# Two fused transformer blocks on one core: linears dealt out over the steps of two attentions, and two orders in layer norm

## Chip, core and metric

One core of a Trainium2 chip runs the whole program. The metric is the device time of one execution in microseconds. Matmuls run on TensorE (PE; its weight loads are PEld), the other engines are VectorE (DVE), ScalarE (ACT), GpSimd (POOL) and SyncE (SP), which issues the DMAs.

## What is computed

Two blocks run one after the other on x of 512 tokens by 1024 channels, all in float32. The change lies in the second block, which has two layers (l = 0, 1). What matters of each, cut from the reference:

```python
proj = x @ w_in
da_q, da_k, da_v, hg_q, hg_ff, hg_fb, hg_i, hg_g, mx_q = jnp.split(proj, split_idx, axis=-1)
...
p = jax.nn.softmax(s, axis=-1)               # differential attention, 4 heads, 512 keys
a = p[:, :, 0] - lam * p[:, :, 1]
return jnp.einsum('bhqk,bkhv->bqhv', a.astype(v.dtype), v)
...
mkv = (mem @ w_mem_kv).reshape(B, M, 2, MX_HEADS, MX_HEAD_DIM)
mx_o = memory_attention(mx_q.reshape(B, S, MX_HEADS, MX_HEAD_DIM), mkv[:, :, 0], mkv[:, :, 1])
...
mix = jnp.concatenate([da_o, hg_o, mx_o], axis=-1) @ w_out
x = layer_norm(DEEPNORM_ALPHA * x + mix, ln1_g, ln1_b)
...
return layer_norm(DEEPNORM_ALPHA * x + ffn, ln2_g, ln2_b)
```

`hg_o` comes from a gated linear recurrence over the tokens, whose inputs are the hg parts of the projection. The memory has 256 rows.

## The kernel before

**Linears.** A float32 product is made of three faster matmuls. A weight block of 128x1024 lands in a ring of nine slots, ACT casts it to its high part WH (`cast_to`, L431), POOL subtracts to get the low part WL (`rest_to`, L442), and PE multiplies WH by the high and low parts of the input and WL by the high part (L490, L491, L493 in `unit_pe`; L468 to L470 where two groups run side by side in `pair_pe`). WH and WL have three places each (`SPLITS`), so the cast of block p waits until PE has used block p - 3. A group of a feature linear is one block: eight values of k, three matmuls of 512 columns each, into one PSUM bank, 24 matmuls in all.

**Order.** Each engine's program is written out by hand in `tensor`, `vector`, `scalar`, `gpsimd` and `sync`, and an engine takes its instructions in that order. Semaphores tie them together. PSUM has eight banks. `bank.take` gives out the one that was taken longest ago, and `bank.claim` sets some aside for a pool of their own, from which `take_in` takes.

**A layer.** `tok_pe` makes q, k and v and turns q and k (L2413), and ACT (L2426) and DVE (L2443) copy the turned tiles. Then comes the differential attention, `diff`: 16 tiles (head by 128 queries) in a pipeline of 20 steps. In step t PE does the values of tile t - 4 (L2485), the turn of tile t - 3 (L2478) and the scores of tile t (L2471). DVE takes the maxima (L2494, L2496) and mixes the two softmaxes (L2499 to L2505), ACT does the two exponentials (L2517), the copy of the turned tile (L2524) and of the values (L2529). Beside it, in every fourth step (`t % 4 == 0`), one whole item of `mem_pe` is put in: for l = 0 first the values of the memory (`mem_values_pe`, L2558), then the four groups of the memory queries (`L_mq`), whose PSUM ACT copies at L2587.

Then `memory`, the attention to the memory: 16 tiles, 19 steps, three short PE stages each: values (L2349), turn (L2322), scores (L2288). DVE takes the maximum (L2294, L2301) and scales the output (L2359, L2362), ACT does the exponential (L2311) and the copy of the turned tile (L2331). Beside it DVE also normalises the differential attention's output (`da_norm_v`, L2629 to L2640, one piece a step for ten steps). PE has nothing beside it. All its scores wait until the last group of queries has been copied (`A.ready`).

Then `recur_in_pe`: twelve groups (`L_hg`) for the recurrence, back to back, whose results ACT puts through silu (L2756) and sigmoid (L2758) and DVE through `gates_v` (L2716 to L2727). The recurrence, the output linear (`mix`), a layer norm, the feed forward part and a second layer norm follow.

**Layer norm.** There are five: `ln_in`, and two a layer. In `spread_v` DVE forms the variance (L881, L884), ACT takes the root (L725) and copies the mean (L896), DVE takes the reciprocal (L887), PE spreads it to all partitions (`whole_pe`, L714), and DVE scales X (L781). The mean is first taken off X: DVE does that for tiles 0 and 1 (`off_v`, L874), POOL for tiles 2 to 7 (L901). `kept_a` (L804) adds the bias to the kept copy of X on ACT, after the high parts (L798). For three of the five, PE has the memory's keys (L2544) or values to compute around L714. For the first norm of layer 1 and the last norm it has nothing.

## Time and profile before

| | before |
|---|---|
| median of 3 runs | 3335.7 us (3334.98 to 3341.27) |
| profiled execution, its own time | 3338.81 us |
| its span, first to last instruction | 3337.0 us |
| TensorE busy | 3234.9 us (97%) |
| weight load / VectorE / ScalarE / GpSimd busy | 77% / 42% / 39% / 40% |
| mean granted TensorE clock | 0.988 |
| DMA | 286.10 MB, mean 86 GB/s |

Busy PE time counts a matmul from its start to a modelled end, and the ends overlap the next start, so the pitch from start to start says more than the duration of one. A bracket at the end of a timeline row is the idle time before it and what ended it.

### The profile page before, as it was taken

How to read it: one execution, taken by the hardware profiler on the slowest of the kernel's cores; microseconds unless marked ns; L12 is line 12 of the kernel's file. 1: busy time of each engine (PE TensorE's matmuls, PEld its weight loads, DVE VectorE, ACT ScalarE, POOL GpSimd, SP SyncE). 2: the span in 40 equal slices, each digit the busy share in tenths (PEclk: the TensorE clock that was granted, in tenths of full speed). 3: DMA queues.
4: the chain of work that ended last, by engine and by line, in shares of the span. 5: the costliest groups of instructions: out<-in, count | busy, mean ns of one | idle time of the engine just before them, and what ended most of it. 6: DMA issues, size and time to landing. Idle time of an engine off the chain costs nothing.

```text
span 3337.0 us, 40463 instructions
## 1 busy us (share of the span) xinstructions
PE 3234.9 (97%) x16396; PEld 2575.0 (77%) x16396; DVE 1409.0 (42%) x2583; ACT 1306.1 (39%) x2312; POOL 1328.1 (40%) x754
## 2 busy tenths in 40 slices
PE   7999999999998999999999899999999999999998
PEld 4866888888874556888886688888887678878886
DVE  5657332222238773321224676242322658344132
ACT  4222332322245664433333535343333543444243
POOL 2221432222243445444552134644455123554446
PEclk9999999999999999999999999999999999999999
DMA  6144222122132001323232020423333111122321
GB/s 253 53 170 183 101 79 74 51 67 70 47 124 87 13 13 53 137 85 111 77 125 71 32 72 9 153 89 100 96 92 111 50 51 52 54 88 81 112 84 56
DMA packets 85639, 286.10 MB, mean 86 GB/s; under 512 B 9771, under 2 KB 10347, under 8 KB 84940
## 3 DMA queue, kind: packets, MB, share of 16 engines
q1 hardware_dynamic: 85452, 283.50, 25.9%
q8 instruction: 130, 2.13, 0.3%
q14 instruction: 57, 0.47, 0.0%
HBM read 281.37 MB, written 2.10 MB: 85 GB/s over the span
## 4 chain that ended last, share of the span: by engine, by line
PE 89%; DVE 6%; ACT 2%; DMA 1%; issue 1%; POOL 0%; SPq 0%; DVEq 0%; ACTq 0%
PE ps L490 21%; PE ps L493 21%; PE ps L491 21%; PE ps L530 2%; PE ps L532 2%; PE ps L531 2%; PE ps L2037 2%; PE ps L2849 1%; PE ps L2107 1%; PE ps L1270 1%; PE ps L2471 1%; PE ps L2485 1%; PE ps L559 1%; PE ps L468 1%; PE ps L469 1%
## 5 line engine op out<-in xcount | busy, mean ns | idle before, releaser
L442 POOL TENSOR_TENSOR WL<-ring,WH 128x1024 fp32r<-128x1024 f32 (+2 forms) x427 | 922.2, 2164 | 1458.0 <-ACT WH L431 1457.7
L490 PE MATMUL ps<-HX,WH 128*128 128x512 f32 x1768 | 694.9, 393 | 3.5 <-POOL WL L442 3.5
L493 PE MATMUL ps<-HX,WL 128*128 128x512 f32 x1768 | 691.7, 391 | 0.0
L491 PE MATMUL ps<-HX,WH 128*128 128x512 f32 x1768 | 690.2, 390 | 0.0
L431 ACT CAST WH<-ring 128x1024 fp32r<-128x1024 f32 (+2 forms) x443 | 420.2, 950 | 374.9 <-PE ps L493 316.8
L490 PE MATMUL ps<-FR,WH 128*128 128x512 f32 x1120 | 418.7, 374 | 0.3
L491 PE MATMUL ps<-FR,WH 128*128 128x512 f32 x1120 | 409.5, 373 | 0.0
L490 PEld LDWEIGHTS ps<-HX,WH 128*128 128x128 f32 x1768 | 332.4, 188 | 82.2 <-issue 6.5
L493 PE MATMUL ps<-FR,WL 128*128 128x512 f32 x1120 | 389.2, 373 | 0.0
L493 PEld LDWEIGHTS ps<-HX,WL 128*128 128x128 f32 x1768 | 333.7, 189 | 49.5
L491 PEld LDWEIGHTS ps<-HX,WH 128*128 128x128 f32 x1768 | 332.7, 188 | 49.3
L954 DVE SCALAR_TENSOR_TENSOR T<-ps,pv,T 128x511 f32<-128x511 f32 (+1 forms) x154 | 109.4, 710 | 499.4 <-ACT T L950 499.3
L490 PEld LDWEIGHTS ps<-FR,WH 128*128 128x128 f32 x1120 | 210.3, 188 | 46.8 <-DVE FR L3062 1.1
L491 PEld LDWEIGHTS ps<-FR,WH 128*128 128x128 f32 x1120 | 210.3, 188 | 37.5
L950 ACT ACTIVATE T<-ps,pv 128x512 f32<-128x512 f32 (+1 forms) x154 | 113.1, 749 | 303.5 <-PE ps L493 290.8
L493 PEld LDWEIGHTS ps<-FR,WL 128*128 128x128 f32 x1120 | 198.6, 188 | 29.8
L909 DVE SCALAR_TENSOR_TENSOR X<-ps,mod,X 128x512 f32<-128x512 f32 x64 | 48.0, 751 | 337.6 <-PE ps L493 320.7
L1593 ACT CAST FR<-T 128x512 fp32r<-128x512 f32 x110 | 61.3, 577 | 248.3 <-DVE T L1621 145.7
L491 PE MATMUL ps<-HC,WH 128*128 128x256 f32 x504 | 141.6, 281 | 0.0
L493 PE MATMUL ps<-HC,WL 128*128 128x256 f32 x504 | 141.4, 281 | 0.0
L490 PE MATMUL ps<-HC,WH 128*128 128x256 f32 x504 | 141.4, 280 | 0.0
L530 PE MATMUL ps<-WH,HX 128*128 128x512 f32 x320 | 126.8, 396 | 0.8 <-ACT AR L2565 0.8
(386 smaller groups left out, 5038.9 us busy)
## 6 DMA issues: line engine op xcount, KB each, us to landing
ring<-in_w_mod SPq DMA_DIRECT2D x96, 512.0 KB, 6.2
ring<-in_ffn_w_up SPq DMA_DIRECT2D x88, 512.0 KB, 3.4
ring<-in_w_up SPq DMA_DIRECT2D x88, 512.0 KB, 3.5
ring<-in_w_in_tok SPq DMA_DIRECT2D x40, 512.0 KB, 3.6
ring<-in_w_in_feat SPq DMA_DIRECT2D x32, 512.0 KB, 3.4
ring<-in_ffn_w_down SPq DMA_DIRECT2D x32, 384.0 KB, 3.1
ring<-in_w_out SPq DMA_DIRECT2D x32, 384.0 KB, 3.1
ring<-in_w_down SPq DMA_DIRECT2D x32, 384.0 KB, 3.2
```

The costliest lines, as they stand in the source:

```text
L431: act.copy(WH[:, p % SPLITS, 0:n], ring.ap(r)).then_inc(*split.a.up("high", p))
L442: pool.tensor_tensor(WL[:, p % SPLITS, 0:n], ring.ap(r), WH[:, p % SPLITS, 0:n], ALU.subtract).then_inc(*ring.frees(r, split.g, "low", p))
L490: pe.matmul(o, high, xh, first, False)
L491: pe.matmul(o, high, xl, False, False)
L493: m = pe.matmul(PS[bs[i]][:, 0:N], low, get(k)[0], False, last)
L530: pe.matmul(PS[bs[t]][:, :], xh[:, tt], high, k == 0, False)
L531: pe.matmul(PS[bs[t]][:, :], xh[:, tt], low, False, False)
L532: m = pe.matmul(PS[bs[t]][:, :], xl[:, tt], high, False, k == 7)
L950: act.activation(dst, src, ACT.Identity, scale=w1, bias=b).then_inc(*steps.up("conv", *name))
L954: dve.scalar_tensor_tensor(dst[:, 1:N], src[:, 0:N - 1], w0, dst[:, 1:N], ALU.mult, ALU.add).then_inc(*steps.up())
L1593: act.copy(hidden(L, n, s)[0], d).then_inc(*fw.a.up("high", L.name, n, s))
L2037: pe.matmul(PS[b][:, 0:c1 - c0], QT[n % 2][0:96, h, t * 128:t * 128 + 128], KT[n % 2][0:96, h, c0:c1], True, True).then_inc(*att.pe.up("sc ...
```

## The change

Six edits, all in how work is ordered:

1. `diff` takes a table `PIECES[l]` that says how many pieces of the work beside it PE does in each of its 20 steps. A piece is one k of a group (three matmuls, `unit_pieces_pe`) or, for l = 0, one of eight pieces of the memory's values. The table of layer 0 gives 2, 1, 1, 1, 1, 1, 1, 0, 2, 2, 2, 2, then 3 a step, 40 pieces in all; that of layer 1 gives 1 to 3 a step, 32 in all. ACT takes its part of a group one step after PE has finished it (`filled`). The scores have a pool of four banks, the work beside two.
2. `memory` gets the first three of the recurrence's twelve groups beside it (`recur_first_pe`), two pieces a step in steps 0 to 7 and one in steps 8 to 15. Their three banks are set aside until the recurrence's input stage, where `recur_in_pe` does the other nine. ACT casts one more block in each of the steps 5, 12 and 18 (`recur_casts_a`).
3. Scores of the memory attention wait for their own head's queries alone (`A.ready(i)`).
4. In `tok_a` the last cast stands behind the four copies of turned keys, and in `mem_a` the cast stands behind the copy and reaches one block further.
5. In `spread_v` DVE takes the reciprocal ahead of the first `off_v`.
6. For the first norm of layer 1, `kept_a` casts two blocks after its first three tiles (`casts` = 2).

```diff
+        def unit_pieces_pe(pe, L, g, stream, b):
...
+            for k in range(k1):
...
+                pe.matmul(o, WH[:, p % SPLITS, c], xh, k == 0, False)
+                pe.matmul(o, WH[:, p % SPLITS, c], xl, False, False)
+                m = pe.matmul(o, WL[:, p % SPLITS, c], xh, False, k == g.kt - 1)
...
+                yield
...
             for j, (k, s) in enumerate(part_items(sts)):
+                if 3 <= j < 3 + casts:
+                    cast_to(act, ring.cast)
...
-            off_v(dve, q, 0)
             dve.wait_ge(*nm.a.at("root", q.name))
             dve.reciprocal(t, t).then_inc(*nm.v.up("inverse", q.name))
+            off_v(dve, q, 0)
             off_v(dve, q, 1)
...
-                for done in A.ready:
-                    pe.wait_ge(*done)
+                pe.wait_ge(*A.ready(i))
...
-            cast_to(act, g.last + 3)
             for h in range(4):
                 act.wait_ge(*da.pe.at("turn", l, h, 1))
...
+            cast_to(act, g.last + 3)
...
-                    b = bank.take("ds", l, i, d)
+                    b = bank.take_in("ds", "ds", l, i, d)
...
+        PIECES = ((2, 1, 1, 1, 1, 1, 1, 0, 2, 2, 2, 2, 3, 3, 3, 3, 3, 3, 3, 3),
+                  (2, 2, 3, 1, 1, 1, 2, 1, 1, 2, 1, 1, 2, 1, 1, 2, 2, 2, 2, 2))
...
-                if t % 4 == 0:
+                for _ in range(turns[t]):
                     next(beside, None)
...
+        def recur_first_pe(pe, l, ready):
+
+            piece = 0
+            for g in L_hg[l].groups[0:3]:
+                b = bank.take_in("first", L_hg[l].name, g.key, 0)
+                for _ in unit_pieces_pe(pe, L_hg[l], g, (hx, S, ready), b):
+                    piece += 1
+                    if piece > 16 or piece % 2 == 0:
+                        yield
+
+        def recur_casts_a(act, l):
+            for t in range(19):
+                if t in (5, 12, 18):
+                    cast_to(act, L_hg[l].groups[(t - 5) // 6].last + 3)
+                yield
```

On PE in the differential attention of layer 0, the order before has 24 matmuls of a group in one block (the first rows of it, after the scores at L2471):

```order
7002 L2478 MATMUL ps<-ident,AR 128x128 x4
7003 L2471 MATMUL ps<-AR 128x512 x2
7004 L490 MATMUL ps<-HX,WH 128x512
7005 L491 MATMUL ps<-HX,WH 128x512
7006 L493 MATMUL ps<-HX,WL 128x512
7007 L490 MATMUL ps<-HX,WH 128x512
```

In the changed kernel every step has two or three pieces (lines are shifted: L2505, L2498, L2491 are values, turn and scores; L508 to L510 a piece):

```order
7038 L2505 MATMUL ps<-AR 128x128 x4
7039 L2498 MATMUL ps<-ident,AR 128x128 x4
7040 L2491 MATMUL ps<-AR 128x512 x2
7041 L508 MATMUL ps<-HX,WH 128x512
7042 L509 MATMUL ps<-HX,WH 128x512
7043 L510 MATMUL ps<-HX,WL 128x512
7044 L508 MATMUL ps<-HX,WH 128x512
7045 L509 MATMUL ps<-HX,WH 128x512
7046 L510 MATMUL ps<-HX,WL 128x512
7047 L2505 MATMUL ps<-AR 128x128 x4
```

The block of 24 is thus dealt out over several steps. On PE in the memory attention of layer 0, two steps before:

```order
7143 L2349 MATMUL ps<-AR 128x128 x2
7144 L2322 MATMUL ps<-ident,AR 128x128 x2
7145 L2288 MATMUL ps<-AR 128x256
7146 L2349 MATMUL ps<-AR 128x128 x2
7147 L2322 MATMUL ps<-ident,AR 128x128 x2
7148 L2288 MATMUL ps<-AR 128x256
```

and one step of the changed kernel, with the start of the next (L2369, L2342, L2308 are values, turn and scores):

```order
7169 L2369 MATMUL ps<-AR 128x128 x2
7170 L2342 MATMUL ps<-ident,AR 128x128 x2
7171 L2308 MATMUL ps<-AR 128x256
7172 L508 MATMUL ps<-HX,WH 128x512
7173 L509 MATMUL ps<-HX,WH 128x512
7174 L510 MATMUL ps<-HX,WL 128x512
7175 L508 MATMUL ps<-HX,WH 128x512
7176 L509 MATMUL ps<-HX,WH 128x512
7177 L510 MATMUL ps<-HX,WL 128x512
7178 L2369 MATMUL ps<-AR 128x128 x2
```

Six matmuls that stood behind the whole stage now stand in each of its first eight steps, three in each of the next eight. On ACT after the first norm of layer 1 (L817 the high parts, L825 `kept_a`, L971 the first convolution of the feed forward part, L431 a cast), changed kernel:

```order
1548 L817 ACTIVATE HX<-X,pv 128x512 x8
1549 L825 ACTIVATE X<-X,pv 128x512 x3
1550 L431 CAST WH<-ring 128x1024
1551 L825 ACTIVATE X<-X,pv 128x512
1552 L431 CAST WH<-ring 128x1024
1553 L825 ACTIVATE X<-X,pv 128x512 x4
1554 L971 ACTIVATE T<-ps,pv 128x512
```

Before, the eight tiles of `kept_a` stood together and the two casts behind the first silu and the first high part of the feed forward stage. The orders of POOL and SP, their instructions and their number are as they were.

## Rows read from the trace of the kernel before

**Rows 1.** The page: busy time of each engine.

```profile
PE 3234.9 (97%) x16396; PEld 2575.0 (77%) x16396; DVE 1409.0 (42%) x2583; ACT 1306.1 (39%) x2312; POOL 1328.1 (40%) x754
```

**Rows 2.** Stretches, memory attention: window, length, busy of PE, PEld, DVE, ACT, POOL, PEclk.

```profile
1871.00:1903.00 32.00, 24.96 (x131) 17.12 (x130) 26.38 (x100) 15.45 (x50) 0.17 (x1) 0.95 0.00 1
...
2676.00:2708.00 32.00, 25.77 (x130) 18.26 (x130) 26.50 (x100) 15.35 (x50) 0.28 (x1) 0.89 0.01 2
```

**Rows 3.** Timeline of PE, layer 0, differential attention: start, duration, instruction, idle before.

```profile
1788.45 1.13 PE L2471 MATMUL ps<-AR 64*128 64x512 f32 x4 [1.59 <-ACT AR L2426]
1789.51 14.00 PE L2558 MATMUL ps<-ring,CX 128*128 128x512 f32 x32
...
1825.67 1.13 PE L2471 MATMUL ps<-AR 64*128 64x512 f32 x4
...
1828.25 1.13 PE L2471 MATMUL ps<-AR 64*128 64x512 f32 x4
1836.33 1.13 PE L2471 MATMUL ps<-AR 64*128 64x512 f32 x4
...
1870.72 1.03 PE L2288 MATMUL ps<-AR 128*128 128x256 f32 x4
```

**Rows 4.** Timeline of PE, layer 1: start of differential attention, start and end of memory attention.

```profile
2605.78 1.13 PE L2471 MATMUL ps<-AR 64*128 64x512 f32 x4 [1.59 <-ACT AR L2426]
2675.61 1.03 PE L2288 MATMUL ps<-AR 128*128 128x256 f32 x4
...
2707.22 0.48 PE L490 MATMUL ps<-HX,WH 128*128 128x512 f32 x1
...
2709.39 0.39 PE L490 MATMUL ps<-HX,WH 128*128 128x512 f32 x1
...
2710.07 0.39 PE L490 MATMUL ps<-HX,WH 128*128 128x512 f32 x1
```

**Rows 5.** Timeline of PE, layer 0, memory attention: one late step and the end.

```profile
1894.21 0.60 PE L2288 MATMUL ps<-AR 128*128 128x256 f32 x2
1894.84 0.71 PE L2349 MATMUL ps<-AR 128*128 128x128 f32 x4
...
1895.61 0.60 PE L2288 MATMUL ps<-AR 128*128 128x256 f32 x2
...
1902.33 0.48 PE L490 MATMUL ps<-HX,WH 128*128 128x512 f32 x1
```

**Rows 6.** Who PE waited for, 1784 to 1904 us: total, times, longest.

```profile
PE ps L2322 <- ACT AR L2311: 5.6, 7, 2.1
PE ps L2349 <- ACT AR L2331: 1.0, 2, 0.6
```

**Rows 7.** Timeline of ACT, layer 0: cast ahead of key copies; a copy in memory attention.

```profile
1785.31 1.08 ACT L431 CAST WH<-ring 128x1024 fp32r<-128x1024 f32 x1
...
1894.41 0.37 ACT L2331 COPY AR<-ps 128x256 f32<-128x256 f32 x1 [0.55 <-PE ps L2322]
```

**Rows 8.** Timeline of DVE and POOL, layer 0: maxima of two steps, and a low part.

```profile
1828.67 0.17 DVE L2496 TENSOR_SCALAR sm<-sm 128x2 f32<-128x2 f32 x1
...
1831.52 2.24 DVE L2496 TENSOR_SCALAR sm<-sm 128x2 f32<-128x2 f32 x1
...
1831.34 2.40 POOL L442 TENSOR_TENSOR WL<-ring,WH 128x1024 fp32r<-128x1024 f32 x1 [42.52 <-ACT WH L431]
```

**Rows 9.** Timeline of ACT, DVE and PE around the first norm of layer 1.

```profile
2947.93 0.31 ACT L725 ACTIVATE T<-T 128x128 f32<-128x128 f32 x1 [0.62 <-DVE T L884]
...
2949.52 0.94 DVE L887 RECIPROCAL T<-T 128x128 f32<-128x128 f32 x1
...
2975.93 0.80 PE L490 MATMUL ps<-HX,WH 128*128 128x512 f32 x1 [2.67 <-POOL WL L442]
```

**Rows 10.** Timeline of POOL and DVE in the last norm: mean off, and scaling.

```profile
3324.18 7.42 POOL L901 TENSOR_TENSOR X<-X,T 128x512 f32<-128x512 f32 x6 [7.79 <-ACT T L896]
...
3326.93 5.45 DVE L3226 SCALAR_TENSOR_TENSOR X<-X,pv,ps 128x512 f32<-128x512 f32 x8 [0.70 <-PE ps L714]
```

More of the change, by code:

```diff
@@ L494, in unit_pe @@
             m.then_inc(*split.pe.up("used", p))
+        def unit_pieces_pe(pe, L, g, stream, b):
+            (p, k0, k1), = g.units
+            get, N, ready = stream
+            assert ring.next() == p
+            pe.wait_ge(*split.g.at("low", p))
+            pe.wait_ge(*bank.free(L.name, g.key, 0))
+            for k in range(k1):
+                c = slice(k * 128, k * 128 + 128)
+                xh, xl = get(k)
+                for done in ready(k):
+                    pe.wait_ge(*done)
+                o = PS[b][:, 0:N]
+                pe.matmul(o, WH[:, p % SPLITS, c], xh, k == 0, False)
+                pe.matmul(o, WH[:, p % SPLITS, c], xl, False, False)
+                m = pe.matmul(o, WL[:, p % SPLITS, c], xh, False, k == g.kt - 1)
+                if k == g.kt - 1:
+                    m.then_inc(*split.pe.up("used", p))
+                yield
         def linear_pe(pe, L, ins, beside=None, groups=None, front=0):
@@ L2573, in mem_pe @@
             if l == 0:
-                mem_values_pe(pe, l)
-                yield
+                yield from mem_value_pieces_pe(pe, l, [bank.take_in("mq", "mv", l, t) for t in range(2)])
             for g in L_mq[l].groups:
-                linear_pe(pe, L_mq[l], lambda g: [(hx, S, ready)], groups=[g])
-                yield
+                b = bank.take_in("mq", L_mq[l].name, g.key, 0)
+                yield from unit_pieces_pe(pe, L_mq[l], g, (hx, S, ready), b)
         def mem_a(act, l):
@@ L2597, in diff, with filled @@
                         run(stage, t - stage)
-                if t % 4 == 0:
+                for _ in range(turns[t]):
                     next(beside, None)
             last_of(beside)
+        def filled(l):
+            turns, n, ends = [0] * 21, 0, list(range(8, 41, 8))[:5 - l]
+            for t, k in enumerate(PIECES[l]):
+                n += k
+                while ends and n >= ends[0]:
+                    turns[t + 1] += 1
+                    ends.pop(0)
+            return turns
         def mem_attention(l):
@@ L2745, in recur_in_pe @@
         def recur_in_pe(pe, l, ready):
-            linear_pe(pe, L_hg[l], lambda g: [(hx, S, ready)])
+            linear_pe(pe, L_hg[l], lambda g: [(hx, S, ready)], groups=L_hg[l].groups[3:])
         def recur_in_a(act, l):
```

45 lines of the change are left out of this document (27 added, 18 removed).

## Prediction

> **What bounds the kernel now.** I read the page first: PE is busy 97% of the span [rows 1]. A kernel in this state gains only where PE waits, or where its busy time is padded. So I went to the timeline of PE in the stages that the change touches, and read pitch, start to start.
>
> In the differential attention the scores of one step start 2.58 us after those of the step before (1825.67 to 1828.25), and 8.08 us after when a group of 24 matmuls lies between (1828.25 to 1836.33) [rows 3]. So a group costs 5.50. A group by itself takes eight k of 0.68 (2709.39 to 2710.07 [rows 4]), that is 5.44, so going in and out of one costs 0.06. DVE needs 2.85 a step (1828.67 to 1831.52) [rows 8], more than PE's 2.58: without a filler DVE falls behind, and in every fourth step a block of 5.5 us lets it catch up again. The stage starts with a wait of 1.59 for the last copy of turned keys [rows 3, 4].
>
> The memory attention is worst. It takes 31.61 us in either layer (1870.72 to 1902.33, 2675.61 to 2707.22) [rows 3 to 5], and its late steps, the best, take 1.40 (1894.21 to 1895.61) [rows 5]. Even those are bound by a chain: the copy of the turned tile ends at 1894.78 [rows 7] and the values start at 1894.84 [rows 5], 0.63 after the scores, although the scores of two tiles in a row are 1.03 long with their modelled end (the first memory row [rows 3]), so that one tile streams for about 0.43. So PE's own work in a step is about 1.40 - 0.20 = 1.20. The early steps wait longer, 5.6 us in seven waits in layer 0 [rows 6], and the granted clock falls to 0.95 and 0.89 in this stage [rows 2], so parts of it run at 1.2 instead of 2.4 GHz. The recurrence's groups behind it run without a gap. They are ready work next to idle time.
>
> **The change part by part.** No arithmetic goes away. Against the profiled execution (3338.8 us, its span 3337.0 and 1.8 around it), with the median of the runs 3.1 below:
>
> *Start of the differential attention.* The cast moved behind the key copies takes 1.08, of which its successor sees some 0.9 [rows 7]. In each layer the wait of 1.59 shrinks by that: 2 x 0.9 = **1.8**. Bounds 0 and 2 x 1.59 = 3.2. I take 0.9, since the last turned tile then becomes the limit. The moved cast is not needed for two more groups; the queued exponential behind it starts later, but the first exponential also waits for DVE's maximum.
>
> *Differential attention.* Layer 0: from 1788.45 to 1870.72 are 82.3 us [rows 3]. PE's own work is 16 x 2.58 = 41.3, the memory's values 13.9 (the 14.0 row less its overlap), four groups of 5.44 = 21.8, in all 77.0: 5.3 of idle and slow time. Layer 1: from 2605.78 to 2675.61 are 69.8 [rows 4], less 41.3 and 21.8: 6.8. In the changed order every step but one has at least one piece, 0.68 (or 1.75 for a piece of the values), so a step lasts 3.26 or more and DVE's 2.85 fits under it, and the last four steps, which have no scores, have two or three pieces. Gain **12.1**. The pool of two banks left for turn and values adds no wait: each reuses a bank whose copy ACT did a step before, and PE needs that copy anyway.
>
> *Memory attention.* 31.6 less 16 steps of 1.20 = 19.2, less 1.0 for the waits of the last three steps, which have no piece (the two waits for L2331 [rows 6]), gives 11.4 a layer, **22.8**. If 1.40 is PE's own pace, it is 16.4. I take 1.20, for the copy that ends just ahead of the values. The three groups' 16.4 us only change place. With two pieces a step lasts 2.56, with one 1.88, and the chain maximum, exponential, turn, copy has that time beside it. The softer wait for the queries matters little, but lets the first scores go while the last queries are copied.
>
> *Going in and out.* PE now visits the filler 19 + 20 + 32 = 71 times instead of 9. 62 x 0.06 = **-3.7** [rows 3]. Bounds 0, and 0.16 a visit (9.9), from the first matmul behind the scores, whose row of 0.48 stands against 0.39 of its followers [rows 4, 5], with 0.06 on top.
>
> *POOL against DVE.* One DVE instruction of 0.17 takes 2.24 in the step in which POOL forms a low part for 2.40 [rows 8]. So each low part can cost DVE 2.1. The Trainium skill ("SBUF — State Buffer", on the port pair that VectorE and GpSimd share) says that the pair is an exclusive lock held for the whole instruction, and the row agrees. This speaks against the change: POOL was idle in the memory attention, 0.17 and 0.28 busy [rows 2], and now forms three low parts in the filled steps of each layer. DVE is busy 26.4 of 32 us there [rows 2]; spread over 37 us of PE work, with three holds of 2.1, it comes to 32.7, which still fits. I charge one hold of the six, as that of step 5 falls among DVE's longest steps: **-2.1**. Bounds 0 and 6 x 2.1 = 12.6. In the differential attention the slack of a step takes them up.
>
> *Layer norm.* The reciprocal can start when the root ends, 2948.24, instead of 2949.52 [rows 9]: 1.2 earlier. In three of five norms PE has other matmuls to do around it, and gains nothing. In the last norm POOL ends its sixth tile at 3324.18 + 7.42 = 3331.60 and DVE's eighth scaling starts at about 3326.93 + 7 x 0.66 = 3331.6 [rows 10]: POOL is the limit, nothing gained. The first norm of layer 1 gains 1.2. There the two early casts also take away the wait of 2.67 at 2975.93 [rows 9]. But ACT now does them ahead of the first convolution, two us later, and the next cast becomes late by a similar chain; I count 1.8 net. Together **3.0**, bounds 0 and 5.6 (1.2, 2.67, and some slow matmuls behind the wait).
>
> Sum: 1.8 + 12.1 + 22.8 - 3.7 - 2.1 + 3.0 = 33.9. 3338.8 - 33.9 = 3304.9 for the profiled execution, **3301.8 for the median**.
>
> **The rivals.**
>
> *A: only listed idle comes back.* PE's 1.40 is its own pace (6.4 less) and a visit costs 0.16 (6.2 more): the gain is 21.3, the time 3314. For it: the timeline lists no idle time of PE in the late steps. Against it: the copy ends 0.06 ahead of the values each time.
>
> *B: POOL holds DVE.* By the skill's rule each hold is paid in full where DVE has no slack. None of the other five in the memory attention is hidden, 10.5 more: the gain is 23.4, the time 3312. For it: 2.24 against 0.17. Against it: the sum of DVE's work above.
>
> *C, slower: five banks are too few.* While three banks hold the recurrence's first groups, values, turn and scores share five. The scores of tile t then take the bank of the values of tile t - 4, so PE waits until DVE has scaled these, and DVE stands in its normalising pieces and POOL's holds. All matmuls queue behind that wait, and the exponentials of ACT behind them. The planned step averages (19.2 + 16.4) / 16 = 2.2 us; the change loses when it averages more than 2.2 + 33.9 / 32 = 3.3. At 3.5 the time is 3301.8 + 32 x 1.3 = 3343. For it: DVE's steps with long pieces approach 3 us. Against it: DVE's busy time, 26.4 over 16 tiles, is 1.65 a tile [rows 2], and the bank has four stages of PE (2.2 us) to come free for a scaling of a third of a microsecond.
>
> *D: no change.* The idle moves behind: the recurrence's input stage waits for DVE and ACT, which now reach their part of it later against PE's, and gives back what was won. Then 3336. Against it: there DVE waits for PE between all gates, so that stage has slack, and its last gate hangs on PE's last group alone.
>
> **How the numbers follow.** Forecast 0.72, A 0.12, B 0.09, C 0.03, D 0.04. What a measurement can tell from no change is 0.2%, 6.7 us. A and B still gain over 20, so faster 0.93, same 0.04, slower 0.03. The bounds of the costs: all at their good end adds 1.4 + 3.7 + 2.1 + 2.6 = 9.8 (3292); the bad ends singly give A and B. For 8 in 10, 3293 to 3315 leaves out C, D and the far ends.
>
> **What would show it.** Right: differential attention of about 78 and 64 us, from first score to first memory score; memory attention of about 37 with 16.4 of it pieces; granted clock near 1 in both; no wait of PE over 0.5 in a filled step; the recurrence's input as before without gaps; the wait at the feed forward's fourth group moved or gone; the last norm unchanged. Wrong: steps of the memory attention over 2.7 with two pieces, waits of PE for DVE L2362 (banks), for DVE's maxima (holds), or for POOL's low parts.

## The result and the profile after

The changed kernel takes **3299.8 us** (median of 4 runs, 3294.27 to 3301.13), the one before on the same chip 3336.5 (4 runs, 3334.98 to 3341.27). The ratio is 0.9884, with a 95% interval of 0.9867 to 0.9902. The ratios of the experiments below are against the kernel before as it ran beside them (medians of 3337.8 to 3339.2). The profiled execution took 3299.9, its span 3298.1 with a mean granted clock of 0.990.

The page of the changed kernel, its first two lines, against [rows 1]:

```profile
span 3298.1 us, 40485 instructions
...
PE 3219.8 (98%) x16396; PEld 2571.5 (78%) x16396; DVE 1406.7 (43%) x2583; ACT 1302.2 (39%) x2312; POOL 1328.8 (40%) x754
```

The five engines have as many instructions as before. PE's busy time fell by only 15 us, the span by 39: more than half of what went was idle time of PE.

The timeline of the changed kernel, PE: the sums of the second block's input norm and of the four norms that follow it (start, duration, engine, line, operation). They cut the program into stretches.

```profile
1700.74 1.02 PE L881 MATMUL ps<-T,ones 128*128 128x512 f32 x2
...
2123.83 0.59 PE L881 MATMUL ps<-T,ones 128*128 128x512 f32 x1
...
2501.22 0.59 PE L881 MATMUL ps<-T,ones 128*128 128x512 f32 x1
...
2910.84 0.59 PE L881 MATMUL ps<-T,ones 128*128 128x512 f32 x1
...
3281.96 0.59 PE L881 MATMUL ps<-T,ones 128*128 128x512 f32 x1
```

I read the same rows in every kernel, and the stages of both attentions (us): the differential attention from its first scores to the first scores of the memory attention, the memory attention from there to the first matmul behind its last values. "Layer 0" and "layer 1" reach from one norm to the next over both attentions and the recurrence; "last part" reaches from the first norm of layer 1 to the last norm. The feed forward part of layer 0 lasts 377.4 in all fourteen kernels of the table.

| kernel | layer 0 | diff. attention | memory att. | layer 1 | diff. attention | memory att. | last part | end |
|---|---|---|---|---|---|---|---|---|
| before | 441.2 | 82.3 | 31.6 | 427.5 | 69.8 | 31.6 | 375.2 | 16.6 |
| changed | 423.1 | 77.2 | 35.8 | 409.6 | 65.0 | 35.8 | 371.1 | 16.1 |
| x1, memory edit undone | 435.2 | 77.2 | 31.5 | 421.6 | 65.0 | 31.5 | 371.1 | 15.9 |
| x2, diff. in blocks | 428.8 | 82.9 | 35.8 | 419.2 | 74.7 | 35.8 | 371.4 | 16.0 |
| x3, norm edits undone | 423.1 | 77.2 | 35.8 | 409.6 | 65.0 | 35.8 | 376.0 | 16.7 |
| x4, memory in blocks | 432.3 | 77.2 | 45.0 | 419.9 | 65.0 | 46.0 | 371.1 | 16.1 |
| x5, four banks | 424.0 | 77.2 | 36.7 | 410.5 | 65.0 | 36.7 | 371.2 | 15.9 |
| x6, three banks | 439.0 | 77.2 | 51.6 | 425.4 | 65.0 | 51.5 | 371.1 | 16.1 |
| x8, casts undone | 423.1 | 77.2 | 35.8 | 409.6 | 65.0 | 35.8 | 374.1 | 15.9 |
| x9, POOL doubled | 425.3 | 77.2 | 38.0 | 411.8 | 65.0 | 38.0 | 371.6 | 16.0 |
| z1, start cast undone | 424.0 | 77.2 | 35.8 | 409.4 | 63.9 | 35.8 | 371.2 | 16.0 |
| z2, more visits | 425.1 | 77.9 | 37.1 | 410.6 | 66.0 | 35.8 | 371.2 | 15.9 |
| y2, lambda first | 423.2 | 77.2 | 35.8 | 409.6 | 65.0 | 35.8 | 371.2 | 16.0 |
| y4, all three | 423.0 | 75.5 | 35.8 + 0.7 | 410.3 | 65.0 | 35.8 + 0.7 | 371.2 | 16.1 |

(In y4 one piece, 0.7, comes behind the last values, and in layer 0 one of 1.8 ahead of the first scores.) Where nothing was changed, layer 0, layer 1 and the stages in them repeat within 0.1 us from run to run. The last part does so within 0.8 (371.1 to 371.6 with the edits of the norms, 375.2 and 376.0 without), and so an edit in it is read less finely. What varies most is the untouched time ahead of the second block's input norm: those sums start at 1699.1 before, at 1700.7 in the changed kernel, and between 1694.9 and 1703.6 in others. So a difference of 1 or 2 us is read from a stretch, and the total can't show it.

Of the 38.9 us by which the span fell, layer 0 gave 18.1, layer 1 17.9, the last part 4.1, the end 0.5, and the first 1700 us took 1.7.

The stages of the changed kernel in windows (columns: window, length, busy time and instructions of PE, PEld, DVE, ACT and POOL, granted clock, DMA share, GB/s); differential and memory attention of layer 0, then of layer 1. The windows over the memory attention answer to [rows 2]:

```profile
1789.25:1866.50 77.25, 77.25 (x385) 50.50 (x386) 48.09 (x116) 42.77 (x107) 10.30 (x4) 1.00 0.15 48
1866.50:1902.30 35.80, 34.79 (x202) 30.23 (x200) 27.89 (x98) 17.78 (x53) 7.20 (x3) 1.00 0.18 59
2588.50:2652.00 63.50, 63.02 (x346) 43.38 (x347) 47.18 (x115) 41.04 (x104) 10.30 (x4) 1.00 0.09 30
2652.00:2689.20 37.20, 36.19 (x208) 31.39 (x207) 28.62 (x98) 17.96 (x54) 7.16 (x3) 1.00 0.15 50
```

The last window holds 1.5 us of the differential attention as well. PE is busy all but 1 us at most in each, and the granted clock is 1.00, so at 2.4 GHz, where it was 0.95 and 0.89 in the memory attention. The waits of PE in both attentions of layer 0 (1784 to 1904), against [rows 6]:

```profile
PE ps L2369 <- ACT AR L2351: 1.0, 2, 0.6
PE ps L2491 <- ACT AR L2445: 0.7, 1, 0.7
```

The 5.6 us of waits of the turns for the exponentials are gone. So are two waits of the differential attention, which the kernel before has in the same stretch and which [rows 6] doesn't show:

```profile
PE ps L2478 <- ACT AR L2517: 2.3, 1, 2.3
PE ps L2485 <- ACT AR L2524: 1.4, 2, 0.7
```

The 1.0 of the two steps without a piece is left, and the wait ahead of the first scores went from 1.59 [rows 3] to 0.72. A step of the memory attention with two pieces, PE alone:

```profile
1872.83 0.60 PE L2308 MATMUL ps<-AR 128*128 128x256 f32 x2
...
1875.31 0.60 PE L2308 MATMUL ps<-AR 128*128 128x256 f32 x2
...
1890.77 0.60 PE L2308 MATMUL ps<-AR 128*128 128x256 f32 x2
...
1892.56 0.60 PE L2308 MATMUL ps<-AR 128*128 128x256 f32 x2
```

Such a step lasts 2.48, and one with one piece (the second pair of rows) 1.79. The difference, 0.69, is a piece; what is left, 1.10, is PE's own work in a step, visit included. The single records agree: two matmuls of scores 0.22 apart, four of values and two of the turn 0.11 apart come to 1.10.

### The profile page after: what moved, and what is told of

Same layout as the page of the kernel before. It is cut to its first block, busy times and chain, and to the rows that moved or that the text cites. A ratio compares the mean times of both kernels' runs of the same rounds, so it can differ in the third digit from the quotient of the medians.

```text
span 3298.1 us, 40485 instructions
## 1 busy us (share of the span) xinstructions
PE 3219.8 (98%) x16396; PEld 2571.5 (78%) x16396; DVE 1406.7 (43%) x2583; ACT 1302.2 (39%) x2312; POOL 1328.8 (40%) x754
## 4 chain that ended last, share of the span: by engine, by line
PE 88%; DVE 5%; ACT 2%; POOL 2%; issue 2%; DMA 1%; SPq 0%; POOLq 0%; DVEq 0%; ACTq 0%
PE ps L490 20%; PE ps L493 20%; PE ps L491 20%; PE ps L549 2%; PE ps L551 2%; PE ps L550 2%; PE ps L2058 2%; PE ps L2900 1%; PE ps L2128 1%; PE ps L1291 1%; PE ps L578 1%; PE ps L468 1%; PE ps L2491 1%; PE ps L469 1%; PE ps L470 1%
## 5 line engine op out<-in xcount | busy, mean ns | idle before, releaser
L490 PE MATMUL ps<-HX,WH 128*128 128x512 f32 x1656 | 650.1, 393 | 1.8 <-POOL WL L442 1.8
L493 PE MATMUL ps<-HX,WL 128*128 128x512 f32 x1656 | 648.2, 391 | 0.0
L491 PE MATMUL ps<-HX,WH 128*128 128x512 f32 x1656 | 646.6, 390 | 0.0
L431 ACT CAST WH<-ring 128x1024 fp32r<-128x1024 f32 (+2 forms) x443 | 420.3, 950 | 375.6 <-PE ps L493 316.8
L490 PE MATMUL ps<-FR,WH 128*128 128x512 f32 x1120 | 419.2, 374 | 0.3
L490 PEld LDWEIGHTS ps<-HX,WH 128*128 128x128 f32 x1656 | 311.2, 188 | 71.2 <-POOL WL L442 3.1
L493 PEld LDWEIGHTS ps<-HX,WL 128*128 128x128 f32 x1656 | 312.3, 189 | 45.0
L491 PEld LDWEIGHTS ps<-HX,WH 128*128 128x128 f32 x1656 | 311.4, 188 | 44.7
L975 DVE SCALAR_TENSOR_TENSOR T<-ps,pv,T 128x511 f32<-128x511 f32 (+1 forms) x154 | 109.4, 711 | 496.0 <-ACT T L971 496.0
L491 PEld LDWEIGHTS ps<-FR,WH 128*128 128x128 f32 x1120 | 210.4, 188 | 37.1
L971 ACT ACTIVATE T<-ps,pv 128x512 f32<-128x512 f32 (+1 forms) x154 | 113.0, 748 | 299.8 <-PE ps L493 287.1
```

The source lines that it names most:

```text
L431: act.copy(WH[:, p % SPLITS, 0:n], ring.ap(r)).then_inc(*split.a.up("high", p))
L490: pe.matmul(o, high, xh, first, False)
L491: pe.matmul(o, high, xl, False, False)
L493: m = pe.matmul(PS[bs[i]][:, 0:N], low, get(k)[0], False, last)
L971: act.activation(dst, src, ACT.Identity, scale=w1, bias=b).then_inc(*steps.up("conv", *name))
L975: dve.scalar_tensor_tensor(dst[:, 1:N], src[:, 0:N - 1], w0, dst[:, 1:N], ALU.mult, ALU.add).then_inc(*steps.up())
```

## The experiments

### One part of the change undone at a time

**x1_memory_undone**: edit 2 alone undone, all twelve groups stand behind the stage again, and ACT's casts beside it (`recur_casts_a`) are gone as well.

```diff
-                bank.claim("first", 3)
-                       recur_first_pe(pe, l, ready))
+                       iter(()))
...
-            linear_pe(... groups=L_hg[l].groups[3:])
+            linear_pe(... groups=L_hg[l].groups)
```

> The changed kernel without its second edit: the twelve groups of the recurrence stand behind the memory attention again, the differential attention stays dealt out. Theory (idle and slow time of PE filled by ready work, stage by stage): the memory attention is as long as before, so 12.2 + 12.2 us of the gain go, and the time is 3299.8 + 24 = 3324, 12 below the kernel before. Rival A (only listed idle comes back): 3299.8 + 17 = 3317. Rival (the two stages' gains are not independent, since a fuller differential attention only hands its work on): over 3330.

Measured: 3320.5 (3318.29 to 3321.97), ratio 0.9943 (0.9926 to 0.9959). By stretches, 12.1 us more in layer 0 and 12.0 in layer 1; the differential attention stays. The waits of PE in the memory attention are back (1862 to 1904):

```profile
PE ps L2342 <- ACT AR L2331: 4.7, 6, 1.2
PE ps L2369 <- ACT AR L2351: 1.0, 2, 0.6
```

The pieces in the memory attention are worth 24.1 us, 62% of the 38.9. The total alone, 20.7 above the changed kernel's, lies between my 24 and rival A's 17; it holds the first 1700 us, which vary by more than the 7 between the two, and the stretches decide.

**x4_memory_in_blocks**: the same three groups inside the memory attention, but eight pieces at once, behind steps 0, 5 and 10.

```diff
-                    if piece > 16 or piece % 2 == 0:
-                        yield
+                    pass
+                for _ in range(5):
+                    yield
...
-                if t in (5, 12, 18):
-                    cast_to(act, L_hg[l].groups[(t - 5) // 6].last + 3)
+                if t in (1, 6, 11):
+                    cast_to(act, L_hg[l].groups[t // 5].last + 3)
```

> The changed kernel with the three groups beside the memory attention each as one block, in steps 0, 5 and 10, and ACT's casts one step behind. Theory: the blocks cover the first wait and let DVE catch up twice, but the 13 steps without a piece go at the chain's 1.40 instead of 1.12, and those in which DVE normalises at DVE's 2.0 to 3.3: some 5 to 7 us a layer slower than the change, 3310 to 3314. Rival (where the pieces stand does not matter, only that PE has other work in the stage): 3300. Rival (a block in the stage stalls the chain behind it, whatever it hides): 3324 as without the edit.

Measured: 3316.4 (3314.59 to 3318.99), ratio 0.9933 (0.9919 to 0.9948); the memory attention is 9.2 and 10.3 us longer than in the changed kernel, more than I had expected. The waits of PE there (1866 to 1915), and a window of it:

```profile
PE ps L2342 <- ACT AR L2331: 3.3, 2, 2.1
PE ps L2369 <- ACT AR L2351: 2.1, 5, 0.6
...
1884.00:1892.00 8.00, 5.86 (x26) 4.61 (x25) 6.67 (x23) 2.71 (x9) 1.32 (x1) 0.79 0.20 66
```

Of the 12.1 us of layer 0 only 2.9 are left when the pieces come in blocks, and of the 12.0 of layer 1 only 1.7. ACT's casts stand in other steps too, but PE waits for no WH or WL there. So it is the dealing out that pays. The listed waits are 5.4; the rest is padded: in the window between two blocks the granted clock is 0.79, part of the time at 1.2 GHz, and steps run at the old pace.

**x2_diff_in_blocks**: the tables of edit 1 give eight pieces in steps 0, 4, 8, 12 (and 16 in layer 0); the other edits stay.

```diff
-        PIECES = ((2, 1, 1, 1, 1, 1, 1, 0, 2, 2, 2, 2, 3, 3, 3, 3, 3, 3, 3, 3),
-                  (2, 2, 3, 1, 1, 1, 2, 1, 1, 2, 1, 1, 2, 1, 1, 2, 2, 2, 2, 2))
+        PIECES = ((8, 0, 0, 0, 8, 0, 0, 0, 8, 0, 0, 0, 8, 0, 0, 0, 8, 0, 0, 0),
+                  (8, 0, 0, 0, 8, 0, 0, 0, 8, 0, 0, 0, 8, 0, 0, 0, 0, 0, 0, 0))
```

> The changed kernel with its table set to whole groups of eight pieces in steps 0, 4, 8, 12 (and 16), as before the change; pools of banks and the memory attention as in the change. Theory: the differential attention is as long as before, 82.3 and 69.8 us, so 5.0 + 4.8 of the gain go: 3309.6. If dealing out does nothing by itself (DVE's lag is hidden anyway): 3300. If the pools of four and two banks cost something where the work is in blocks: over 3313.

Measured: 3315.0 (3313.18 to 3317.93), ratio 0.993 (0.9915 to 0.9944). Layer 0 is 5.7 longer, as the recovered idle predicts, but layer 1 is 9.6 longer, and its differential attention (74.7) lasts 4.8 longer than before the change (69.8). The timeline of x2 around the longest wait of PE in it:

```profile
2600.95 1.05 ACT L431 CAST WH<-ring 128x1024 fp32r<-128x1024 f32 x1
...
2602.07 2.34 POOL L442 TENSOR_TENSOR WL<-ring,WH 128x1024 fp32r<-128x1024 f32 x1 [5.14 <-ACT WH L431]
2602.84 1.59 DVE L2516 TENSOR_SCALAR sm<-sm 128x2 f32<-128x2 f32 x1
...
2604.47 0.69 ACT L2537 ACTIVATE AR<-ps,sm 128x512 f32<-128x512 f32 x1 [2.48 <-DVE sm L2516]
...
2605.93 1.12 PE L2498 MATMUL ps<-ident,AR 128*128 128x128 f32 x4 [3.59 <-DVE AR L2525]
```

The cast that edit 4 moved behind the copy starts POOL's low part just when DVE forms the scale of the maxima: an instruction that takes 0.17 elsewhere takes 1.59, the exponential is late, and PE waits 3.59 for the mixed tile. The kernel before has a wait of 2.2 in this stage for the mixed tile too, so this one explains 1.4 of the 4.8. Behind it the granted clock is lower: 0.72 from 2600 to 2612, against 0.86 in the 12 us around the wait before the change (2612 to 2624). The rest is not traced. So undoing edit 1 alone is not "before": the place of the cast costs something where no piece stands in the next steps.

The total lies above 3313, which I had kept for pools of banks that cost something. PE lists no wait for a bank in either layer (its waits are for mixed and turned tiles and for the first keys), which speaks against it; no run separates the pools from the rest, and the 0.7 by which layer 0's differential attention exceeds the kernel before (82.94 against 82.27) stays open.

**x3_norms_undone** (edits 5 and 6 undone) and **x8_casts_undone** (edit 6 alone):

```diff
 # both kernels
-                ln_a(act, ln_1[l], ..., 2 * l)
+                ln_a(act, ln_1[l], ..., 0)
 # x3 also
+            off_v(dve, q, 0)
             dve.wait_ge(*nm.a.at("root", q.name))
             dve.reciprocal(t, t).then_inc(*nm.v.up("inverse", q.name))
-            off_v(dve, q, 0)
```

> The changed kernel without the edits 5 and 6 (reciprocal behind the first off_v again, no cast within kept_a). Theory, from the stretch between the sums of the first and the second norm of layer 1, 375.2 before and 371.2 after: 4.0 slower than the change, 3303.8, and the stretch at 375.2 again. My prediction's term said 3.0. Rival (that stretch gained from elsewhere, a state of the chip): 3300.

> The changed kernel with the two casts of the first norm of layer 1 back behind all eight convolutions; the early reciprocal stays. Theory: the stretch from that norm's sums to the last norm's sums, 371.1 in the changed kernel and 376.0 with both edits undone, comes to about 374.8: 3.7 for the casts (the wait of 2.67 and slow matmuls behind it) and 1.2 for the reciprocal. Rival: the wait only changes place when ScalarE takes the casts first, so the casts give 1 us or less, and the stretch is 372. In the whole time 3 to 4 us, or 1.

Measured: x3 3302.7 (3301.27 to 3305.3), x8 3299.1 (3296.83 to 3304.62): the totals hardly tell. The last part does: 371.1 changed, 374.1 without the casts, 376.0 without both. So the casts are worth 3.0, where I had expected 3.7. The 1.9 of x3 against x8 is not the reciprocal's alone: in the 20 us behind the norm's sums the granted clock is 0.74 in x3 and 0.91 in x8 and in the changed kernel, and x3's last part is 0.8 longer than that of the kernel before (clock 0.83), though both have the same order there. What the reciprocal does by itself is in PE's wait for it, 2.27 in x3 and 1.04 with the edit: 1.2. The end is 0.6 shorter with it (16.1 against 16.7). In x8 the wait for POOL is there at its full length (first row, 2934.94); in the changed kernel a shorter one is left (second fence, with the reciprocal and PE's wait for it):

```profile
2934.94 0.80 PE L490 MATMUL ps<-HX,WH 128*128 128x512 f32 x1 [2.70 <-POOL WL L442]
```

```profile
2913.96 0.95 DVE L907 RECIPROCAL T<-T 128x128 f32<-128x128 f32 x1 [0.38 <-ACT T L744]
...
2914.97 1.16 PE L733 MATMUL ps<-T,ident 128*128 128x128 f32 x8 [1.04 <-DVE T L907]
...
2949.98 0.50 PE L490 MATMUL ps<-HX,WH 128*128 128x512 f32 x1 [1.05 <-POOL WL L442]
```

The rival that the wait only changes place holds in part: 2.67 [rows 9] became 1.05. The reciprocal itself takes 0.95 behind a wait of 0.38.

### Rival C: how few banks will do

**x5_four_banks** and **x6_three_banks** withhold one and two banks more.

```diff
                 bank.claim("first", 3)
+                bank.claim("aside", 1)   # x6: 2
```

> The changed kernel with one more bank withheld in the memory attention: values, turn and scores share four banks instead of five. Theory (banks come free well before they are needed): the turn of tile t-2 now takes the bank of the values of tile t-4, which VectorE has one step less one matmul to scale; 0 to 4 us above the changed kernel, memory attention 36 to 38 us a layer. Rival C (the banks are what nearly binds): every step now waits for a scaling, 0.5 us or more in each of 32 steps, so 16 us or more above it.

> The changed kernel with two more banks withheld: three banks rotate, so the scores of tile t take the bank of the scores of tile t-1 and wait for its exponential, and the values wait for the scaling of the tile before. Theory: the chain scores, maximum, exponential is about 2.2 us; a step with two pieces (2.48) hides it, one with one piece (1.79) is short by some 0.5, and the three steps at the end too: 5 to 15 us above the changed kernel, and the waits stand in the late steps. Rival C: with five banks it is already close, so each bank less costs like the one before, 30 us or more here, and all of the gain goes.

Measured: x5 3298.0 (3297.38 to 3301.96), ratio 0.9884 (0.9869 to 0.9899), the memory attention 0.9 longer a layer; x6 3330.4 (3327.12 to 3332.8), ratio 0.9975 (0.9966 to 0.9985), 15.8 longer a layer. With four banks rival C is refuted, since it wanted 16 us there. With three, its number (30 or more) is the right one, and my 5 to 15 is wrong. A step of x6:

```profile
1885.27 0.37 ACT L2351 COPY AR<-ps 128x256 f32<-128x256 f32 x1 [2.83 <-PE ps L2342]
...
1885.54 0.48 ACT L2331 ACTIVATE AR<-ps,sm 128x256 f32<-128x256 f32 x1
...
1886.16 0.70 PE L2308 MATMUL ps<-AR 128*128 128x256 f32 x2 [0.93 <-ACT AR L2331]
```

My expectation summed the length of the chain scores, maximum, exponential and let the pieces hide it. But ACT takes the copy of the turned tile t-2 ahead of the exponential of tile t-1, and PE makes that turn in this very step, behind the pieces. So turn, copy, exponential and scores stand in series in every step, and no piece lies beside them. The scores wait 0.93 in 13 steps of a layer (12.1 us), and a step with two pieces lasts 3.68 in place of 2.48. Here the order on ACT sets the need for banks, not the length of a chain. The granted clock stayed at 1.00 over these 51.5 us, with PE busy 74%:

```profile
1864.00:1915.50 51.50, 38.03 (x200) 30.43 (x199) 27.27 (x98) 17.29 (x53) 7.17 (x3) 1.00 0.13 42
```

### Rival B: POOL's holds

**x9_pool_doubled**: POOL forms four low parts a layer twice. Three of them fall into the memory attention; the fourth starts 0.5 us behind its end (1901.00 against 1900.50).

```diff
                 pool.wait_ge(*split.a.at("high", p))
+                if p in [L_hg[l].groups[k].last for l in range(2) for k in range(2, 6)]:
+                    pool.tensor_tensor(WL[...], ring.ap(r), WH[...], ALU.subtract).then_inc(*split.g.up())
+                    pool.wait_ge(*split.g.now())
                 pool.tensor_tensor(WL[...], ring.ap(r), WH[...],
```

> The changed kernel in which POOL forms the low part of the recurrence's groups three to six (of both layers) twice, the second time over the first: VectorE is held twice as long in the memory attention, four times a layer. Theory (holds are hidden in the slack of the steps; only one in six shows): PE sees nothing or up to one hold a layer, 0 to 5 us more in the whole. Rival B (each hold is paid in full): 2.1 us for each doubled low part, 8 x 2.1 = 17 us more.

Measured: 3302.4 (3300.54 to 3305.22), ratio 0.9897 (0.9881 to 0.9914). Layer 0 is 2.2 longer and layer 1 2.2, where payment in full would give 8.4 a layer. One wait per layer makes it:

```profile
1876.20 2.39 POOL L443 TENSOR_TENSOR WL<-ring,WH 128x1024 fp32r<-128x1024 f32 x1 [6.68 <-ACT WH L431]
...
1876.99 4.73 DVE L2695 SCALAR_TENSOR_TENSOR AR<-AR,sm,rows 128x128 f32<-128x128 f32 x4
...
1878.66 2.38 POOL L446 TENSOR_TENSOR WL<-ring,WH 128x1024 fp32r<-128x1024 f32 x1
...
1882.89 0.44 PE L2346 MATMUL ps<-ident,AR 128*128 128x128 f32 x2 [1.72 <-ACT AR L2335]
```

Four DVE pieces that take 1.13 take 4.73 under a double hold. In the changed kernel the single one makes them 2.54, and PE doesn't wait:

```profile
1880.15 2.39 POOL L442 TENSOR_TENSOR WL<-ring,WH 128x1024 fp32r<-128x1024 f32 x1 [9.42 <-ACT WH L431]
...
1880.94 2.54 DVE L2691 SCALAR_TENSOR_TENSOR AR<-AR,sm,rows 128x128 f32<-128x128 f32 x4
```

So the holds are real, and in the changed kernel a step with two pieces hides one: its steps stay at 2.48 around this row. Even the one hold that I had charged is not paid. But x9 doesn't show that doubled holds are hidden. Most of them have nothing to hold. The third low part of the changed kernel, with what DVE does inside it:

```profile
1894.61 2.38 POOL L442 TENSOR_TENSOR WL<-ring,WH 128x1024 fp32r<-128x1024 f32 x1 [12.07 <-ACT WH L431]
...
1894.98 0.42 DVE L2314 TENSOR_REDUCE sm<-ps 128x1 f32<-128x256 f32 x1 [0.23 <-PE ps L2308]
...
1896.19 0.35 DVE L2382 TENSOR_SCALAR AR<-ps,sm 128x128 f32<-128x128 f32 x1 [0.53 <-PE ps L2369]
```

The maximum and the scaling read PSUM, and neither is longer than elsewhere (0.42 and 0.35). Only the normalising pieces, which read two operands from SBUF, are held: by the first low part one of 0.68, which takes 1.63, by the second the four above, by the third none. Of the four doublings of a layer, the one at 1876.20 adds 2.2 to DVE's work in the stage (4.73 against 2.54), the one at 1864.30 adds 0.2, the others nothing, and the layer is 2.2 longer. What was added and met DVE was thus paid nearly in full, and both my theory and the 17 us of rival B counted holds that don't exist.

### Two terms of the sum by themselves

**z1_start_cast_undone**: the first half of edit 4 undone.

```diff
+            cast_to(act, g.last + 3)
             for h in range(4):
                 act.wait_ge(*da.pe.at("turn", l, h, 1))
...
-            cast_to(act, g.last + 3)
```

> The changed kernel with the cast of the next group back ahead of the copies of the turned keys; all else stays. Theory: in layer 0 the first scores wait 0.9 longer (1.6 in place of 0.72). In layer 1 the cast only changed its place in front of the exponential of lambda, which waits for it either way, and the maxima of tile 0 wait for lambda; the 0.40 that the scores of tile 2 wait there for a bank goes, so the stretch from the norm's sums to the sums of the next norm grows by 0.9 in layer 0 and by about 0 to 0.5 in layer 1. Rival (the term as it was predicted): 0.9 in both layers. In the whole 1 to 2 us, which the stretches show and the total time hardly does.

Measured: 3298.2 (3296.46 to 3299.52). Layer 0 is 0.9 longer, layer 1 0.2 shorter, as the theory says and not as the term did. In z1 the first scores of layer 1 wait 1.59, but those of tile 2 do not wait; in the changed kernel they wait for tile 0's exponential and its bank:

```profile
2588.26 1.05 ACT L431 CAST WH<-ring 128x1024 fp32r<-128x1024 f32 x1
...
2589.33 1.28 ACT L2449 ACT_TABLE_LOAD   x1
...
2590.86 0.92 DVE L2474 TENSOR_TENSOR sm<-sm 128x1 f32<-128x1 f32 x1 [2.18 <-ACT sm L2449]
...
2593.39 0.69 ACT L2537 ACTIVATE AR<-ps,sm 128x512 f32<-128x512 f32 x1 [2.57 <-DVE sm L2516]
...
2594.23 1.79 PE L2491 MATMUL ps<-AR 64*128 64x512 f32 x4 [0.40 <-ACT AR L2537]
```

The four matmuls take 1.79 in place of 1.13, so a part of the wait stands within the group; by the stage it is 1.1 in all (65.0 against 63.9). In layer 0 the pieces of the first steps are those of the memory's values, two of them in step 0, longer than the 0.7 of others, and cover it.

**z2_more_visits**: from step 4 on, one piece of a step with two or more (`early`) is taken between values and turn.

```diff
+                def run(stage, i):
+                    da_pe(pe, l, stage, i)
+                    if stage == 4 and early[i + 4]:
+                        next(beside)
```

> The changed kernel, with one piece of each differential step that has two or more taken between the values and the turn instead of behind the scores: the same matmuls, with 12 more goings in and out in layer 0 and 8 more in layer 1. As the term was predicted (0.06 a visit): 0.7 and 0.5 us longer. By its upper bound (0.16): 1.9 and 1.3. As I read the changed kernel's trace (steps equal to their parts, so that a visit costs nothing): 0 in both, or a gain or loss from the other place alone, under 0.3.

Measured: 3302.5 (3301.02 to 3304.84). Layer 0 is 2.0 longer and layer 1 1.0, near the upper bound's 1.9 and 1.3, where I had expected under 0.3. But a step lasts the same (z2, scores to scores with an extra visit between):

```profile
1831.57 1.13 PE L2491 MATMUL ps<-AR 64*128 64x512 f32 x4
...
1834.23 0.48 PE L508 MATMUL ps<-HX,WH 128*128 128x512 f32 x1
...
1835.54 1.13 PE L2491 MATMUL ps<-AR 64*128 64x512 f32 x4
```

3.97, and 3.97 in the changed kernel as well (1832.05 to 1836.02). The last four steps of layer 0 have an extra visit each and last as long as in the changed kernel, too. Of the extra time, 1.3 stand in the memory attention of layer 0, where no visit was added: four steps are longer, each ahead of the turn, which needs the exponential, 0.6 us of it listed as waits. 0.45 is a wait ahead of a piece at 1818.35 for the copies of the memory's values. The 1.0 of layer 1 stands in its last four steps, 0.5 of it a wait for a turned tile; the other 0.5 is not traced, and four extra visits lie there. So a visit costs nothing that a step shows.

### An attempt at a better version

**y2_lam_first** puts the start cast behind the exponential of lambda. **y4_all_three** adds to that 5 steps of two and 14 of one in the memory attention, and one piece ahead of the first scores.

```diff
-            cast_to(act, g.last + 3)
             act.wait_ge(*da.v.at("lam sums", l))
             act.activation(sm[:, 76:78], sm[:, 76:78], ACT.Exp).then_inc(*da.a.up("lam", l))
+            cast_to(act, g.last + 3)
 # y4 also
-                    if piece > 16 or piece % 2 == 0:
+                    if piece > 10 or piece % 2 == 0:
...
+                next(beside)      # ahead of diff, one piece less in its step 0
```

> The changed kernel with that cast moved once more, behind the exponential of lambda. Theory: in layer 1 the exponential of lambda starts 1.05 earlier, and with it the maxima and the first exponential, so that the wait of 0.40 of the scores of tile 2 goes, and up to 1.1 us of the layer's stretch; in layer 0 nothing. The low part of POOL that held a VectorE instruction of the lambda chain falls behind it. Rival: the cast is then late for POOL's low part and PE waits for it at the second group of the queries: a new wait on WL, and nothing or less than nothing gained.

> A version meant to beat the changed kernel: (1) the 24 pieces of the memory attention as 5 steps of two and 14 of one, so that the last three steps have one as well; (2) the cast behind the exponential of lambda; (3) one piece of the filler ahead of the first scores of the differential attention, where PE waits 0.72. Theory: (1) takes away waits of 0.55 and 0.46 a layer, 2.0 in all, if one piece covers the early steps as it covers the late ones; (2) up to 1.1 in layer 1; (3) 0.7 a layer. Together 3 to 4.5 us, so 3295 to 3297 where the changed kernel has 3299. Rival: with one piece from step 5 on, the chain maximum, exponential, turn with VectorE's long pieces beside it does not fit in 1.79 in the early steps, and PE waits there; (1) loses 2 us or more, and the version is no faster.

Measured: y2 3296.2 (3294.89 to 3302.67), ratio 0.9877 (0.9862 to 0.9892); y4 3299.6 (3295.18 to 3300.2), ratio 0.9883 (0.9867 to 0.99). By stretches neither gains: 423.2 and 409.6 for y2, 423.0 and 410.3 for y4. Each edit meets the same thing. In y2 the cast is later, so POOL's low part now falls on the scale of tile 0's maxima:

```profile
2593.88 2.37 POOL L442 TENSOR_TENSOR WL<-ring,WH 128x1024 fp32r<-128x1024 f32 x1 [8.47 <-ACT WH L431]
...
2594.47 1.80 DVE L2516 TENSOR_SCALAR sm<-sm 128x2 f32<-128x2 f32 x1
```

In y4 the two waits at the end of the memory attention are gone (1.0 a layer), but the step under the first hold has one piece and no longer hides it, and the stage with its last piece is 0.7 longer:

```profile
1874.83 2.54 DVE L2691 SCALAR_TENSOR_TENSOR AR<-AR,sm,rows 128x128 f32<-128x128 f32 x4
...
1878.54 0.44 PE L2342 MATMUL ps<-ident,AR 128*128 128x128 f32 x2 [1.43 <-ACT AR L2331]
```

The piece ahead of the first scores wins about as much in layer 0, which comes out even (423.0); in layer 1 it wins nothing, since tile 2's listed wait for its bank grows from 0.4 to 1.1. Both rivals were right in the outcome and not in the way: PE waits for no WL in y2, and y4's waits cost 0.7 a layer, not 1 or more. No version here beats the changed kernel. A table that gives two pieces just to the steps under a hold, and one to the rest with three at the end, was not tried.

## Why the prediction was right, and where its terms were off

The forecast was 3304.9 for a profiled execution and 3301.8 for the median; measured 3299.9 and 3299.8. The mechanism was the forecast's: idle and slow time in both attentions comes back when pieces cover every step. That the medians agree within 2.0 is in part luck. I had set the median 3.1 below the profiled execution, as it lay before the change; after it both are the same, which hides 3 of the 5.0 us by which the forecast of the profiled execution was off. And misses of both signs cancel in the sum. By terms, with the visits (0.06 each) and the charged hold put to the stage that they were for:

| term | predicted | measured |
|---|---|---|
| start of differential attention | 1.8 | 1.7 (0.87 in each layer) |
| differential attention, with 30 visits | 12.1 - 1.8 = 10.3 | 9.8 (5.0 and 4.8) |
| memory attention, with 32 visits and a hold | 22.8 - 1.9 - 2.1 = 18.8 | 24.4 (12.2 and 12.2, from the end of the one attention to the first group left) |
| layer norm | 3.0 | 4.6 (4.1, and 0.5 at the end) |
| ahead of the second block's input norm | 0 | -1.7 (untouched, varies by more) |
| sum | 33.9 | 38.9 (terms rounded) |

- **Memory attention**, the largest miss, 5.6 us. The prediction took PE's own step as 1.20 and a visit as 0.06; the step measures 1.10 with its visit, 32 x 0.16 = 5.1 us less. The choice between 1.20 and 1.40 went the right way but not far enough. The 0.20 that I took off the 1.40 was the idle time between scores and values alone. The first matmul of the values behind it is padded as well: in the kernel before it starts at 1894.84 and the second at 1895.05, 0.21 apart, where the others are 0.11 apart. With the hold that was not paid (2.1) the two come to 7.2, and 1.6 of it was lost again: 0.3 in one step a layer (1.96 and 1.91 in place of 1.79), some 0.5 by pieces of 0.69 instead of 0.68 (an estimate from these rows), the rest not traced.
- **Going in and out**: predicted -3.7, measured nothing (z2). The 0.06 had been read from 5.50 against 5.44 for a whole group, two sums of pitches from different stages; this is too small a difference to carry 62 times.
- **POOL against DVE**: predicted -2.1, measured 0 in the changed kernel. Three holds of 2.1 in each memory attention, as the prediction counted them, don't exist: two low parts a layer meet an instruction that they hold, for 1.0 and 1.4, and the third meets none. A second hold behind the first costs 2.2 a layer (x9), one hold in a step with one piece 1.4 (y4), and in x2 the wait behind one on a chain without a piece is 3.6, 1.4 more than stood there before. The exclusive lock which the Trainium skill describes ("SBUF — State Buffer", "Who interferes with whom") is met there by VectorE instructions with two SBUF inputs, or in a two-port mode, and not by `tensor_reduce`. The rows agree: a `tensor_scalar` of 0.17 from SBUF to SBUF (128x2) became 1.59, 1.80 and, before, 2.24, the maxima and what reads PSUM stayed as they were. Whether a hold is paid depends on the pieces beside it.
- **Start**: right at the place, but the 0.9 of layer 1 is given back at the scores of tile 2 (z1: 1.1). "the queued exponential behind it starts later, but the first exponential also waits for DVE's maximum" was the step that failed: DVE's maximum waits in its program behind lambda, and lambda for the cast. In all this term is worth 0.9 - 0.2 = 0.7, not 1.8; the differential attention of layer 1 without that wait would have gained 5.9, nearer to its 6.8.
- **Layer norm**: 1.8 for the casts were 3.0, and the 1.2 for the reciprocal is borne out by PE's wait, 2.27 less 1.04; by the stretch 1.1 is left of the 4.1 beside the casts. The wait that I let come back is 1.05. That POOL limits the last norm is right: its six tiles take 7.41, DVE waits for them twice, and ACT's last row ends 12.8 us behind the norm's sums in both kernels. The end still gained 0.5, behind that row, and why is open.
- **Rivals.** A is out, since PE's step is under even the lower of its two prices. B is out for the changed kernel, whose steps stay at 2.48 around the longest hold; x9 doesn't refute it, since there the one doubling that held DVE for long was paid. C is out by x5: four banks cost 0.9 a layer. D is out: nothing behind the stages gave back what they won: undoing edit 2 moves the stage and the layer by the same 12 us.
- **What would show it**: differential attention 77.2 and 65.0 (78 and 64 expected), memory attention 35.8 (37), clock 1.00, the waits gone, the later wait moved. Not foreseen were the 0.4 for tile 2's bank, though under the 0.5 allowed, and the end, which was to stay as it was.

## What to carry over

Pieces of independent work are worth most when every step of a latency-bound stage has one: in three blocks the same work gave 2.9 and 1.7 us in the two layers, dealt out 12.1 and 12.0. Lay the larger portions where another engine is known to be held, since a small portion there gives its gain back (y4), and read first which of its instructions are held at all (x9); and when a chain seems hidden, follow each engine's program order for its members, not the sum of their lengths (x6, z1). Where a total scatters by several us, measure an edit between two anchors that it can't touch on either side, and compare the granted clock there: in the attentions these repeated within 0.1 us, behind a layer norm, where the clock differed, within 0.8.

## What was unexpected of the hardware

- The granted clock stays at 1.00 (2.4 GHz throughout) in x6 with PE busy 38.0 of 51.5 us, its waits 0.9 at most; it is 0.79 (in part 1.2 GHz) in the window of x4 in which PE is busy 5.86 of 8 us, behind waits of up to 2.1. An equal busy share had a different clock. What decides it was not tested here.
- POOL's low part holds only some of DVE's instructions. In the whole changed kernel 40 instructions of L975, which take one operand from PSUM (128x511), start inside a low part, and none is longer than the 0.75 of those outside; all 14 of L2772 that start inside one, from SBUF to SBUF (128x512), take about 2.6 in place of 0.43.
- Two instruction streams of different kinds (turns of float32 tiles and the products of split weights) can be changed over on PE 16 more times with no difference in their steps, 3.97 us both ways in those of two pieces; at four more places, the last steps of layer 1, the stage grew by 1.0, half of it a listed wait.
- The untouched first half of the program varies by up to 8.7 us from one run to the next (1694.9 to 1703.6), while each later stretch repeats within 0.1, the last part within 0.8. The granted clock goes with it at both ends: 0.98 over the first 1690 us in y2, where they are longest, 0.99 in x8, where they are shortest.
